# Triangular inverses on four quarters of the array, and a new order of work in the second scan

## What is computed

```
def gated_delta_chunked(q, k, v, g, beta):          # first scan, 4 heads of 128
    ...
    kk = jnp.einsum('nbhid,nbhjd->nbhij', kc, kc)
    a_mat = jnp.where(strict, bc[..., :, None] * kk * gamma, 0.0) + jnp.eye(C, dtype=q.dtype)
    u = lax.linalg.triangular_solve(a_mat, bc[..., None] * vc, left_side=True, lower=True)
    w = lax.linalg.triangular_solve(a_mat, (bc * jnp.exp(G))[..., None] * kc, left_side=True, lower=True)
    qk = jnp.einsum('nbhid,nbhjd->nbhij', qc, kc) * gamma
    def step(S, inp):
        v_new = u_i - jnp.einsum('bhcd,bhde->bhce', w_i, S)
        ...
def rwkv7_scan(r, decay, k, v, kk, a):              # second scan, 8 heads of 64
    def step(S, inp):
        sa = jnp.einsum('bhvk,bhk->bhv', S, -kk_t)
        S = (S * w_t[:, :, None, :] + sa[..., None] * (kk_t * a_t)[:, :, None, :]
             + v_t[..., None] * k_t[:, :, None, :])
        return S, jnp.einsum('bhvk,bhk->bhv', S, r_t)
```

## Time and profile before

| | us |
|---|---|
| median of three executions (4394.19 to 4404.03) | 4396.11 |
| profiled execution | 4381.25 |
| its span, first to last instruction | 4379.4 |
| first scan in it, from 242 to 574 | 332 |
| second scan in it, from 755 to 1283 | 528 |
| PE busy in the span | 3800.6 |
| DVE busy in the span | 2186.5 |

### The profile page before, as it was taken

How to read it: one execution, slowest core, us unless ns; L and a number is a source line. 1 busy time by engine, 2 the same in 40 slices (tenths; PEclk the granted TensorE clock), 3 DMA queues, 4 the chain that set the end, 5 groups by cost and what they waited for, 6 DMA issues and landing times.

```text
span 4379.4 us, 52302 instructions
## 1 busy us (share of the span) xinstructions
PE 3800.6 (87%) x21059; PEld 2135.3 (49%) x21059; DVE 2186.5 (50%) x4388; ACT 1035.7 (24%) x2734; POOL 816.8 (19%) x860
## 2 busy tenths in 40 slices
PE   7988898888889777777777777689999999989999
PEld 4556665888874433333233222355555444444444
DVE  4845434656554667677677544553332026533321
ACT  2422222333321223323323322321110011511100
POOL 1033300323320133333333333100000000000000
PEclk8999998899899899999999999899999999999999
DMA  4145520000021399999999999701111111012221
GB/s 160 56 185 219 196 76 8 2 2 2 2 74 58 133 420 420 420 420 418 420 419 406 421 420 420 288 21 39 58 58 39 53 57 58 1 40 77 77 72 72
DMA packets 167088, 743.00 MB, mean 170 GB/s; under 512 B 12022, under 2 KB 58369, under 8 KB 91840
## 3 DMA queue, kind: packets, MB, share of 16 engines
q0 software_dynamic: 77264, 549.79, 30.5%
q1 hardware_dynamic: 89008, 187.77, 12.0%
q10 hardware_dynamic: 576, 2.10, 0.1%
HBM read 737.52 MB, written 2.10 MB: 169 GB/s over the span
## 4 chain that ended last, share of the span: by engine, by line
PE 62%; DMA 20%; DVE 12%; ACT 4%; issue 2%; POOL 0%; DVEq 0%; ACTq 0%; POOLq 0%
PE bank L104 34%; DMA row<-in_experts,idxs 10%; DMA wring<-in_experts,idxs 9%; PE bank L2478 9%; PE bank L2459 5%; PE bank L949 4%; DVE junk L2364 2%; DMA wring<-in_ada_w 1%; PE bank L551 1%; PE bank L1567 1%; DVE TTm L1002 1%; PE bank L1597 1%; PE bank L958 1%; DVE TT L1009 0%; PE bank L1589 0%
## 5 line engine op out<-in xcount | busy, mean ns | idle before, releaser
L104 PE MATMUL bank<-h2T,wring 128*128 128x512 f32 (+1 forms) x2112 | 759.9, 523 | 0.0
L2459 PE MATMUL bank<-row,dg 128*128 128x512 f32 x1224 | 592.9, 632 | 183.6 <-ACT dg L2435 183.2
L104 PEld LDWEIGHTS bank<-h2T,wring 128*128 128x128 f32 x2112 | 402.8, 191 | 355.8 <-issue 337.5
L2364 DVE CUSTOM_DVE_ANT_0 junk<-row,bank 128x1024 f32<-128x1024 f32 x306 | 373.6, 1221 | 251.6 <-DMA row<-in_experts,idxs 238.3
L2459 PEld LDWEIGHTS bank<-row,dg 128*128 128x128 f32 x1224 | 235.5, 201 | 540.0 <-issue 540.0
L2459 PE MATMUL bank<-wring,dg 128*128 128x512 f32 x824 | 394.0, 625 | 119.3 <-ACT dg L2435 119.3
L2478 PE MATMUL bank<-wring,gT 128*128 128x512 f32 x880 | 383.1, 598 | 8.6 <-DVE gT L2876 8.6
L2350 POOL DMA_INDIRECT row<-in_experts,idxs x306 | 294.5, 962 | 473.5 <-PE bank L2459 467.6
L2364 DVE CUSTOM_DVE_ANT_0 junk<-wring,bank 128x1024 f32<-128x1024 f32 x206 | 251.5, 1221 | 174.0 <-DMA wring<-in_experts,idxs 166.0
L2459 PEld LDWEIGHTS bank<-wring,dg 128*128 128x128 f32 x824 | 156.5, 198 | 354.1 <-issue 353.9
L2865 DVE TENSOR_SCALAR cv<-pad,fp 128x769 f32<-128x769 f32 (+1 forms) x88 | 54.2, 615 | 509.7 <-ACT pad L2831 509.7
(11 more groups left out here) (545 smaller groups left out, 4945.9 us busy)
## 6 DMA issues: line engine op xcount, KB each, us to landing
wring<-in_ada_w SPq DMA_DIRECT2D x36, 2048.0 KB, 8.4
wring<-in_ffn_w_up SPq DMA_DIRECT2D x44, 1024.0 KB, 7.6
wring<-in_ffn_w_down SPq DMA_DIRECT2D x8, 2048.0 KB, 7.7
wring<-in_w_in SPq DMA_DIRECT2D x7, 2048.0 KB, 8.0
wring<-in_peer_w_query SPq DMA_DIRECT2D x4, 2048.0 KB, 8.0
wring<-in_ffn_w_down SPq DMA_DIRECT2D x4, 1536.0 KB, 6.8
wring<-in_attn_w_qkv SPq DMA_DIRECT2D x3, 2048.0 KB, 8.1
row<-in_experts,idxs POOLq DMA_INDIRECT x306, 17.6
```

Of the source, the lines that this page charges most:

```text
L104: ins = e.matmul(out, l, r, start=(start and n == 0), stop=(stop and n == len(pairs) - 1))
L2364: e.tensor_tensor_reduce(self.junk, self.ring[j % self.ROWS][:, 0:1024], P.pairs[b % 2], 1.0, 0.0, MUL, ADD, self.dots[:, b % 2, x:x + 1]) ...
L2459: ins = e.matmul(ks[half], self.dg[u % 4], self.ring[u % self.ROWS][:, 1024 + half * 512:1536 + half * 512], start=(x == 0), stop=(x == 127))
```

## The change

Four things change.

1. In TYT the two products of a unit are interleaved and go to different quarters: TY from input half a to output half b, YT from a to a, so that four matmuls in a row name four quarters. TY and YT have a PSUM bank each (banks 2q and 2q+1), and the same two banks serve all products of the inverse of unit q. `Tm`, `Y`'s partner, lies with its halves exchanged for this.
2. All other products of the first scan rotate over three banks (4 to 6; 7 remains with the mods), those of the second scan over four (4 to 7).
3. VectorE forms `TD` from `AT` itself, no longer from ScalarE's copy. In the second scan `AT` is in PSUM, and its bank becomes free when ScalarE has copied `OFF` (`ac_off`), which now waits for VectorE's first inverse.
4. The second scan's order is written out. `AT` of chunk u+1 stands ahead of Y of level 5 of chunk u, BT, Qb and Qk of chunk u between its levels 1 and 4, and pieces of the chain of u-1 and of the preparation of u+1 stand between all groups of the levels.

```diff
     def bank(self, pe, *user):
         n = self.turn % self.ring
         self.turn = n + 1
-        return self.own(pe, n, *user)
+        return self.own(pe, self.low + n, *user)
...
-    def pairs(self, e, k, l, r):
+    def level(self, pe, u, s):
+        P, e, w = self.P, pe.e, self.w
+        ty, yt = P.own(pe, self.A, "TY", u, s), P.own(pe, self.B, "YT", u, s)
         for h in range(4):
-            for a in (slice(0, 64), slice(64, 128)):
-                ins = e.matmul(k[a, h * 64:(h + 1) * 64], l[a, h, :], r[a, h, :], start=True, stop=True)
-        return ins
+            for a, b in self.halves:
+                e.matmul(ty[b, h * 64:(h + 1) * 64], w["TD"][a, h, :], w["Y"][a, h, :], start=True, stop=True)
+                ins = e.matmul(yt[a, h * 64:(h + 1) * 64], w["Y"][a, h, :], w["TD"][a, h, :], start=True, stop=True)
+        ins.then_inc(*self.st.T.up("TYT", u, s))
...
+    def dv_first(self, dv, u, src, given):
+        P, e, w, V = self.P, dv.e, self.w, self.st.V
+        dv.wait_ge(*P.at(*given))
+        dv.wait_ge(*V.now())
+        m0 = self.mask(0)
+        for a, _ in self.halves:
+            e.tensor_tensor(w["TD"][a], src[a, :, a], m0[a], MUL).then_inc(*V.up())
+        dv.wait_ge(*V.now())
+        e.tensor_tensor(w["TD"], over4(P.id64), w["TD"], SUB).then_inc(*V.up("TT", u, 0))
...
+    def ac_off(self, ac, u, src, free, over):
+        P, e, w, A, lo, hi = self.P, ac.e, self.w, self.st.A, self.lo, self.hi
+        ac.wait_ge(*P.at("TT", u, 0))
+        if over:
+            ac.wait_ge(*P.at(*over))
+        e.activation(w["OFF"][hi], src[lo, :, hi], ACT.Copy).then_inc(*A.up(*free))
...
 class GdnScan(Stage):
...
-        P.ring = 7
+        P.low, P.ring, P.turn = 4, 3, 0
...
 class RwkvScan(Stage):
     def pe(self, pe):
...
-            chain = self.chain_pe(pe, u - 1) if u else iter(())
-            next(chain, 0)
-            in_turn(chain, self.inv[u][0].pe(pe, ("r", u, 0)), self.inv[u][1].pe(pe, ("r", u, 1)),
-                    self.prepare_pe(pe, u + 1) if u < 11 else iter(()))
+            more, x = u < 11, ORDER[u // 6][u % 6] >= 2
+            level = [self.inv[u][q].pe(pe, self.tag(u, q)) for q in range(2)]
+            for g in last:
+                next(g)
+            if more:
+                self.decay_pe(pe, u + 1)
+            for g in last:
+                next(g)
+            if more:
+                self.rate_pe(pe, u + 1)
+            self.both(level)
+            if u:
+                self.x_pe(pe, u - 1)
+            self.both(level)
+            if u:
+                self.sa_pe(pe, u - 1)
+            self.both(level)
+            self.product_pe(pe, u, "BT", "ka2", "al")
...
+            if more:
+                self.product_pe(pe, u + 1, "AT", "be", "al")
+            self.both(level)
+            if more:
+                self.turned_pe(pe, u + 1, "be", "bet")
+            self.both(level)
+            if more:
+                self.turned_pe(pe, u + 1, "ka2", "kat")
+            last = level
...
     def ac(self, ac):
...
+            for s in (2, 3, 4):
+                for i, n in inv:
+                    i.ac_y(ac, n, s)
+            if u < 11:
+                self.in_ac(ac, u + 1)
+            for i, n in inv:
+                i.ac_y(ac, n, 5)
```

More of the change, by code:

```diff
@@ L1050, in ac @@
         A.mark("TT", u, 6)
+    def ac(self, ac, u):
+        yield
+        for s in range(1, 6):
+            self.ac_y(ac, u, s)
+            yield
+            yield
+        self.ac_y(ac, u, 6)
+        yield
+        self.ac_u(ac, u)
         yield
@@ new lines, in pe, with both, product_pe @@
+        self.both(last)
+        self.both(last)
+        self.x_pe(pe, 11)
+        self.sa_pe(pe, 11)
+        for _ in self.y_pe(pe, 11):
+            pass
+        self.T.mark("chain", 11)
+        P.low, P.ring = 0, 8
+    def both(self, gens):
+        for g in gens:
+            next(g)
+    def product_pe(self, pe, u, name, l, r):
+        P, e, w = self.P, pe.e, self.ops[u]
+        ks = [P.bank(pe, name, u, q) for q in range(2)]
+        pe.wait_ge(*P.at("r_ops_bk" if r == "al" else "r_ops", u))
+        for x in range(4):
+            for q in range(2):
+                pp = slice(q * 64, q * 64 + 64)
+                ins = e.matmul(ks[q][:, x * 128:(x + 1) * 128], w[l][pp, x, :], w[r][pp, x, :], start=True, stop=True)
+        ins.then_inc(*self.T.up(name, u))
@@ L1626, in dv @@
         e.memset(self.S, 0.0).then_inc(*V.up())
[L1627 removed]
+        for _ in self.prepare_dv(dv, 0):
+            pass
         for u in range(12):
[L1629 to L1631 removed]
+            x = ORDER[u // 6][u % 6] >= 2
+            make = self.prepare_dv(dv, u + 1) if u < 11 else iter(())
             if u >= 2:
                 dv.wait_ge(*P.at("chain", u - 2))
[L1634 removed]
+            if u % 6 < 2:
@@ new lines, in dv @@
+            next(make, 0)
+            for q in range(2):
+                self.inv[u][q].dv_turn(dv, self.tag(u, q), ("Yps", self.tag(u - 1, q), 6) if u else None)
+            next(make, 0)
+            self.levels_dv(dv, u, 1)
+            self.keep_dv(dv, u, "BT")
+            self.levels_dv(dv, u, 2)
+            next(make, 0)
+            if u:
+                self.y_dv(dv, u - 1)
+            self.levels_dv(dv, u, 3)
+            if u:
+                self.state_dv(dv, u - 1)
+            next(make, 0)
@@ new lines, in dv, with levels_dv, keep_dv @@
+            if x:
+                self.keep_dv(dv, u, "Qb")
+            self.levels_dv(dv, u, 4)
+            if x:
+                self.keep_dv(dv, u, "Qk")
+            next(make, 0)
+            self.levels_dv(dv, u, 5)
+        self.y_dv(dv, 11)
+    def levels_dv(self, dv, u, s):
+        for q in range(2):
+            self.inv[u][q].dv_level(dv, self.tag(u, q), s, ("SA", u - 2) if u >= 2 else None)
+    def keep_dv(self, dv, u, name):
+        P, e, V, d = self.P, dv.e, self.V, u // 6
+        keep = over(P.stri[d], 4) if name == "BT" else over(P.inc[d].bitcast(U32), 4)
+        dv.wait_ge(*P.at(name, u))
+        for q in range(2):
+            e.copy_predicated(self.res[u % 2][q][name], keep, v4(P.ps(name, u, q))).then_inc(*V.up("free", name, u, q))
+        V.mark("free", name, u)
@@ L1739, in prepare_dv @@
+            masks = [self.inv[u][q].po(po, self.tag(u, q), ("Yps", self.tag(u - 1, q), 5) if u else None) for q in range(2)]
+            for n in range(2):
+                for g in masks:
+                    next(g)
+            next(make, 0)
+            for n in range(6):
+                for g in masks:
+                    next(g)
+            next(make, 0)
     def prepare_dv(self, dv, u):
```

375 lines of the change are left out of this document (199 added, 176 removed).

## The result

The changed kernel takes 4340.52 us (median of 9 runs, 4333.41 to 4364.43) where the kernel before took 4394.19 on the same chip (9 runs, 4365.67 to 4404.03): a ratio of 0.9898, interval 0.9869 to 0.9927 (the ratio follows the means, 4344.35 and 4388.98; the medians by themselves give 0.9878). It is faster, by 1.0%; the forecast was 2.4%. The profiled execution is 45.8 us shorter than that of before (4333.6 for 4379.4 us), where the forecast had 106. Of these, 43.9 us lie in the two scans, 22.5 us in the first and 21.4 in the second; the stretches ahead of the scans, between them and behind them are within 4 us of what they were.

What follows compares the result with a forecast made beforehand. TensorE was taken as the bound in both scans. Second scan -80 us (68 at equal clock, 12 of clock) and first scan -26 made -106, from the profiled 4381.25 to 4275, 4290 on the median's scale; range 4238 to 4365.

Steps and rivals of the forecast that it cites:

- Four quarters: Inverse levels of both scans: TY and YT overlap on four quarters, a unit's TYT falls from 0.93 to 0.47 us.
- the rival without overlap: Both scans: the four quarters don't overlap, TYT stays at 0.93 us; -34 us, 4362 us; chance 0.10.
- What they are worth: The quarters' saving: 4.7 us of a steady second-scan chunk; 12 us of a possible 28 in the first scan.
- The order of the second scan: Second scan: the new order saves 2.2 us per steady chunk beside the quarters; chunk 36.5 us instead of 43.4.
- some 3 us stay idle ahead of the decay: Steady second-scan chunk: a 12.5 us chain against 9.4 us of TensorE's work leaves some 3 us idle.
- The clock of the second scan: Second scan: of 42 us lost to the clock, 6 go as the stage shrinks and another 6 through denser work.
- Slower, by the clock: Second scan: the wait ahead of the decay drops the clock in every chunk; 4422 us at 30 us each; chance 0.05.
- the 5.2 us idle of the chunk at 0.99: Argument against the slower rival: a steady second-scan chunk ran at nearly full clock despite 5.2 us of TensorE idle time.
- The first scan: First scan: -26 us, from quarters 12, step-end waits 10 and clock 4; bounds +6 and -61.
- What would show it: Signs in both scans: TYT 0.47 us, second scan some 448 us, first-turn waits under 1.5, mean clock at least 0.91.
- the sign of being wrong: Both scans: TensorE's records in a level no closer than 29 ns, or a mean clock under 0.85.
- the slack is taken elsewhere: Weights' DMA holds the first scan, VectorE makes the steady second-scan chunk 38.5 us; -72 us, 4324 us; chance 0.25.

Runs made afterwards that it cites:

- e7: e5 with all TY of a unit issued before all YT, meant to leave two quarters running at once; 4302.45 us, ratio 0.9821 to the kernel before.
- e10: e5 with every matmul of TY and YT issued twice into the same place, on four quarters, in both scans; 4365.99 us, ratio 0.9956.
- e1: The changed kernel with its second scan's bank ring skipping AT's two banks, so the decay doesn't wait for them; 4316.76 us, ratio 0.9843.
- e5: The changed kernel with AT's two banks skipped and two unneeded 128x512 matmuls ahead of each decay in the second scan; 4283.24 us, ratio 0.9768.
- e3: The changed kernel with all TY of a unit issued before all YT, in both scans; 4384.03 us, ratio 1.0004 to the kernel before.
- e2: The changed kernel with two unneeded 128x512 matmuls ahead of the decay in the second scan, the bank wait left in; 4322.55 us, ratio 0.985.
- e6: The kernel before with two unneeded 128x512 matmuls ahead of product SA in each of the second scan's 12 chunks; 4377.72 us, ratio 0.9982.
- e11: e5 with one unneeded 128x512 matmul ahead of each decay instead of two; 4301.43 us, ratio 0.9812 to the kernel before.
- e12: e1 with two unneeded 128x512 matmuls behind the rate, ahead of the first turn, in eleven chunks; 4312.25 us, ratio 0.9828 to the kernel before.

## Why the prediction was half right

In the profiled executions 45.8 us were won; forecast 106. Step by step:

- **Four quarters.** Right. TYT of a unit spreads over 0.47 us, the rival without overlap is out.
- **What they are worth.** The second scan was to give 4.7 us a chunk, some 55 in all; the runs show 31 (e7) to 45 (e10) at equal clock. The first scan was to give 12; e7 and e10 show 8 to 12.
- **The order of the second scan.** Forecast 13 us beside the quarters. The whole scan at equal clock went from 478.5 (517.4 - 0.44 x 88.5) to 423.1 (496.0 - 0.44 x 165.7), 55 us for the forecast 68, so 10 to 24 are the order's, as the quarters take 45 or 31. The steady chunk takes 37.5 at equal clock, for the forecast 36.5. The step "some 3 us stay idle ahead of the decay" was right in kind and in place; the waits were 1.2 us in seven chunks and 5.5 in three, 24.8 together, and cost 16 (e1).
- **The clock of the second scan: the step that failed.** The prediction said: "The 42 us lost to the clock shrink with the stage by 6 (42 x 68 / 528); another 6 I count as given back, since the work stands denser." (The first sum gives 5.4, not 6.) The work doesn't stand denser: TensorE is busy for 88.5% of the scan before and 88.1% now, and idle for 59 us in both. In place of -12, half clock rose by 77 us and took 34. The 46 us between -12 and +34 are most of the 60 that were missed; the 13 of the step above are nearly all of the rest. e5 shows it by taking half clock away: with 8.9 us of it the ratio is 0.9768, where the forecast was 0.9759. (That e5 meets the forecast so well is in part luck: it also lacks the decay's wait, 16 us, and has 21 us of idle matmuls.) The clock stood among my rivals ("Slower, by the clock", chance 0.05), but by a wait that doesn't bring it by itself: I named the one ahead of the decay, and e1, without it, has the same 166 us at half clock. My argument against the rival, the 5.2 us idle of the chunk at 0.99, was no test either: the sum of a chunk's idle time says little, since before and now TensorE is idle for the same 59 us and half clock is 88.5 and 165.7. What the runs do show is that in the changed kernel and in e1 the clock falls behind the waits at the last products (18 of the 19 stretches that the two sections above count), which come to 11 us in every version, and that other work right behind these waits takes the falls away. Why the new order has more half clock than the old stays open beyond that.
- **The first scan.** Forecast -26, measured -22.5. The waits of its first turns fell from 23.5 to 13.1 us, 10.4 for the forecast 10, though the longest is 4.4 and not under 1.5. The wait for the weights rose from 7.6 to 14.5, as expected in kind. The clock brought nothing (47.0 and 45.6 us at half) where I had 4.
- **What would show it.** The mean clock of the second scan, 0.83, is under the 0.85 that I had named as the sign of being wrong.

The time, 4340.52, lies nearest the rival "the slack is taken elsewhere" (4324), for the most part not for its reason. At equal clock the steady chunk takes 37.5 us, halfway from the forecast 36.5 to that rival's 38.5; the larger part of what was missed, 46 us, is the clock's. That the time falls inside the stated range says nothing for the sum: the range reached down to the case in which the quarters don't overlap, and they do.

Open: whether the 9 and 27 us of "issue" in e10 are late instructions; why the first scan's half clock doesn't answer to filled waits; why the new order, and e3 more so, has more half clock than the old with the same waits at the last products; and whether the idle matmuls of e5 help by their place or by their shape, since no run put other work there. Half clock in a scan comes from one profiled execution of each kernel and moves by some 20 us by itself; the steps from before to after, from after to e3 and from e1 to e5 (77, 56 and 157 us) are well beyond that, and the mean clocks of the timed executions go the same way.

## What to carry to other kernels

When TensorE is the bound, price a reordering twice: by the idle time it removes, and by the clock, which this prediction sized at -12 us and which took 34. Short waits at the end of a loop body cost this kernel more by the clock than by their length: half clock cost the scan 73 us (165.7 x 0.44), the wait ahead of the decay 16. If the waits can't be removed, a little idle work right behind them can pay for itself, and it has to be tried, not argued: 21 us of unneeded matmuls brought 48 us net (e1 to e5), and the version with them and without the bank wait beats both kernels, at 4283.24 us for 4384.7. Its place has to be tried too: the same matmuls a little later left 101 us at half clock. And an experiment that undoes a change must be measured for what it undid, as e3 and e7 show.

## What the runs showed of the hardware

- Matmuls on other quarters start ahead of older ones: in e7 YT began when 6 of TY's 16 records had yet to start, and 1.86 us became 1.35.
- Four matmuls that share rows and columns of the array in pairs start within 0.02 us, every 58 ns. The mean distance of two starts is 15 ns.
- Half clock doesn't follow TensorE's busy time, nor its idle time. From after to e3 TensorE's busy time in the scan rose from 437 to 484 us and its half clock from 166 to 221 us; from e1 to e5 21 us of added work took it from 166 to 9. TensorE's waits at the last products came to 11.0 to 11.8 us in before, after, e1, e2, e5, e6, e11 and e12, with 9 to 166 us at half clock.
- Half clock costs 0.44 us for each us of it in these scans: six executions of the same first scan, with 45.6 to 66.8 us of it, agree within 2.1 us by this price.
- An unneeded matmul of 128x512 in float32 shows as two records and takes 1.06 us of TensorE's busy time at full clock, five times the price that I gave it for e6 (0.43 us for two).
